# A streaming-encoder block with seven products in its up projection: moves between partition groups issued by GpSimd, turns and taps placed some blocks later

## The reference

```
h = rmsnorm(x, g_ffn_pre[l])
u = causal_dwconv(h @ w_up[l], ffn_conv_w[l])
gate, val = jnp.split(u, 2, axis=-1)
x = x + rmsnorm((jax.nn.silu(gate) * val) @ w_down[l], g_ffn_post[l])
```

## Time and profile before

| | us |
|---|---|
| median of 3 runs | 1702.69 |
| lowest, highest | 1702.57, 1703.47 |
| the profiled execution | 1708.27 |
| its span, first to last instruction | 1706.2 |
| TensorE busy in the span | 1648.2 |
| VectorE busy | 1094.3 |
| ScalarE busy | 834.0 |
| GpSimd busy | 54.2 |

### The profile page before, as it was taken

The page is one execution under the profiler, slowest core; times in us unless marked ns, Lnnn a source line. Parts: engine busy times, 40 slices in busy tenths (PEclk is TensorE's granted clock), DMA queues, the critical chain, the costliest instruction groups (busy, mean ns, idle before and its releaser), DMA issues.

```text
span 1706.2 us, 22099 instructions
## 1 busy us (share of the span) xinstructions
PE 1648.2 (97%) x7219; PEld 1344.5 (79%) x7219; DVE 1094.3 (64%) x1500; ACT 834.0 (49%) x1075; POOL 54.2 (3%) x117
## 2 busy tenths in 40 slices
PE   9999999999999999999999988988889899999998
PEld 7888888888888888888888766766667688888886
DVE  5655566555666676666666777777787777753544
ACT  6644344444444444444456555554545555543432
POOL 2500000000000000000000000000000000000000
PEclk9999999999999999999999999999999999999999
DMA  8877767777666756766664655655556577755653
GB/s 281 274 219 220 195 180 208 213 220 209 189 205 191 260 186 199 235 215 215 227 217 136 192 176 173 206 175 172 176 170 208 163 236 232 246 190 178 210 195 137
DMA packets 207792, 346.81 MB, mean 203 GB/s; under 512 B 28953, under 2 KB 52330, under 8 KB 207210
## 3 DMA queue, kind: packets, MB, share of 16 engines
q1 hardware_dynamic: 201033, 342.48, 64.5%
q0 software_dynamic: 2048, 2.10, 0.4%
q10 hardware_dynamic: 4640, 1.33, 0.3%
HBM read 318.02 MB, written 2.10 MB: 188 GB/s over the span
## 4 chain that ended last, share of the span: by engine, by line
PE 78%; SPq 8%; DVE 4%; DMA 4%; issue 3%; ACT 2%; DVEq 0%; ACTq 0%; POOL 0%; POOLq 0%
PE PS L1679 21%; PE PS L1680 21%; PE PS L1681 21%; SPq L507 7%; DMA raw<-in_w_up_dram 3%; PE PS L1811 3%; PE PS L1813 3%; PE PS L1812 3%; DVE w_lo L1586 2%; ACT w_hi L1005 2%; SPq L522 1%; PE PS L1895 1%; PE PS L1896 1%; PE PS L1897 1%; DVE value_conv L1432 1%
## 5 line engine op out<-in xcount | busy, mean ns | idle before, releaser
L1098 DVE TENSOR_TENSOR w_lo<-raw,w_hi 128x1024 fp32r<-128x1024 f32 x439 | 534.8, 1224 | 451.5 <-ACT w_hi L653 450.3
L653 ACT ACTIVATE w_hi<-raw 128x1024 fp32r<-128x1024 f32 x439 | 462.3, 1059 | 535.4 <-PE PS L1681 453.7
L1679 PE MATMUL PS<-w_hi,hT_hi 128*128 128x512 f32 x1312 | 516.8, 394 | 6.5 <-DVE w_lo L1586 6.4
L1680 PE MATMUL PS<-w_lo,hT_hi 128*128 128x512 f32 x1312 | 511.5, 390 | 0.0
L1681 PE MATMUL PS<-w_hi,hT_lo 128*128 128x512 f32 x1312 | 511.5, 390 | 0.0
L1679 PEld LDWEIGHTS PS<-w_hi,hT_hi 128*128 128x128 f32 x1312 | 246.3, 188 | 72.2 <-DVE w_lo L1586 16.7
L1681 PEld LDWEIGHTS PS<-w_hi,hT_lo 128*128 128x128 f32 x1312 | 246.4, 188 | 52.2
L1680 PEld LDWEIGHTS PS<-w_lo,hT_hi 128*128 128x128 f32 x1312 | 246.5, 188 | 48.6
L1586 DVE TENSOR_TENSOR w_lo<-raw,w_hi 128x1024 fp32r<-128x1024 f32 x136 | 164.9, 1218 | 70.0 <-ACT w_hi L1005 70.0
L1005 ACT ACTIVATE w_hi<-raw 128x1024 fp32r<-128x1024 f32 x136 | 136.7, 1048 | 75.5 <-DMA raw<-in_w_up_dram 50.2
L1679 PE MATMUL PS<-w_hi,act_hi 128*128 128x512 f32 x336 | 131.0, 390 | 0.0
(11 more groups left out here) (251 smaller groups left out, 1807.7 us busy)
## 6 DMA issues: line engine op xcount, KB each, us to landing
raw<-in_w_up_dram SPq DMA_DIRECT2D x176, 512.0 KB, 4.0
raw<-in_w_in_dram SPq DMA_DIRECT2D x112, 512.0 KB, 4.1
raw<-in_w_gate_dram SPq DMA_DIRECT2D x96, 512.0 KB, 4.6
raw<-in_w_down_dram SPq DMA_DIRECT2D x88, 512.0 KB, 4.4
raw<-in_w_mem_kv_dram SPq DMA_DIRECT2D x32, 512.0 KB, 6.3
raw<-in_w_o_dram SPq DMA_DIRECT2D x32, 512.0 KB, 4.5
up_moved<-up_stage SPq DMA_DIRECT2D x352, 32.0 KB, 2.8
raw<-in_w_conv_out_dram SPq DMA_DIRECT2D x16, 512.0 KB, 3.7
```

The lines of the kernel that those rows point to most:

```text
L653: nc.scalar.activation(w_hi[i % RING][:], raw[i % RING][:], ACT.Copy).then_inc(hi_ready, inc)
L1098: nc.vector.tensor_tensor(w_lo[i % RING][:], raw[i % RING][:], w_hi[i % RING][:].bitcast(F32), ALU.subtract).then_inc(lo_ready, inc)
L1679: nc.tensor.matmul(o, a_hi, b_hi, start=first, stop=False, skip_group_check=onto)
L1680: nc.tensor.matmul(o, a_hi, b_lo, start=False, stop=False, skip_group_check=onto)
```

## The change

All moves of the up projection leave SyncE's queue and are issued by GpSimd: chunk 0 written out, chunks 1 to 10 in a hardware loop, each half as one group of 16 DMAs behind its two waits. SyncE's loop has loads alone. In the fast chunks the turns, taps, product and rounding are done behind other units: the product and `act_lo` of chunk `jp` leave the round of `j` and are done at the start of the next one, where they are `value_done(jp - 1, 6)` and `(jp - 1, 7)`. Chunk 9 does those of chunk 7. The silu of the gate, the gate's evacuation and the value's first tap stand behind units 8 and 9.

```diff
@@ fast_step, the loads @@
                 for m, (kb, half) in enumerate(((0, 0), (0, 1), (1, 1), (1, 0))):
                     fast_load(j, m, m - 3 if first else (-4, -3, -2, 0)[m], kb, half)
-                    move_squares(jp, 0, m)
                 for m in range(4, 2 * CB):
                     half, kb = (0, m - 2) if m < CB + 2 else (1, m - CB)
                     fast_load(j, m, (3, 5, 6, 6)[m - 4] if m < 8 else m, kb, half)
-                    if CB <= m < CB + P // SQ:
-                        move_squares(jp, 1, m - CB)
@@ GpSimd @@
+            def move_squares(j, half):
+
+                pool.wait_ge(up_out, 2 * j + half + 1)
+                if not isinstance(j, int):
+                    pool.sem_inc(norm_pace, 1)
+                    pool.wait_ge(up_turned, 2 * j + half - 1)
+                    pool.sem_inc(norm_pace, 1)
+                for a in range(P // SQ):
+                    for m in range(P // SQ):
+                        pool.dma_start(up_moved[half][SQ * m:SQ * (m + 1), a, :, :].rearrange("p q n -> p (q n)"),
+                                       up_stage[half][SQ * a:SQ * (a + 1), m, :, :, :].rearrange("p b t n -> p (b t n)")).then_inc(up_in[half], 16)
+
+            move_squares(0, 0)
+            move_squares(0, 1)
+            with pool.Fori(1, NUP) as j:
+                move_squares(j, 0)
+                move_squares(j, 1)
@@ ScalarE, up_step of chunk 9 @@
                         split(n, i, up_landed(j, i))
+                        if jp == FAST_END - 1 and i == 1:
+                            value_done(jp - 1, 7)
                         gate_done(jp, i)
@@ ScalarE, fast_step @@
-                    if s in (1, 4):
-                        gate_done(jp, {1: 3, 4: 6}[s])
-                    if s in (6, 10):
-                        value_done(jp, {6: 3, 10: 7}[s])
-                    if s == 8:
+                    if s == 1 and not first:
+                        value_done(jp - 1, 7)
+                    if s in (5, 8):
+                        gate_done(jp, {5: 3, 8: 6}[s])
+                    if s == 9:
                         up_evacuate(j, 0)
+                        value_done(jp, 3)
@@ VectorE, up_step of chunk 9 @@
+                        if jp == FAST_END - 1 and i in (1, 2):
+                            value_done(jp - 1, i + 5)
@@ VectorE, fast_step @@
-                    if s in (0, 2, 3):
-                        gate_done(jp, {0: 2, 2: 4, 3: 5}[s])
-                    if s in (5, 7, 8, 9, 11):
-                        value_done(jp, {5: 2, 7: 4, 8: 5, 9: 6, 11: 7}[s])
+                    if s in (0, 2) and not first:
+                        value_done(jp - 1, {0: 6, 2: 7}[s])
+                    if s in (4, 6, 7):
+                        gate_done(jp, {4: 2, 6: 4, 7: 5}[s])
+                    if s in (8, 10, 11):
+                        value_done(jp, {8: 2, 10: 4, 11: 5}[s])
```

21 lines of the change are left out of this document (1 added, 20 removed).

## The result

The changed kernel takes 1679.76 us (median of four executions, 1678.81 to 1681.73) beside 1702.63 us for the kernel before (four, 1701.0 to 1703.47). The ratio is 0.9869, with an interval of 0.9856 to 0.9881: 22.9 us faster. The prediction was 1658.0 with a range of 1651 to 1676. The direction was right and the size was not: half of the gain that was worked out is there, and the time lies above the range.

A forecast was written before the change was run, and what follows sets the result against it. TensorE, 97% busy, was taken to wait 39.0 us before Y, seven times. Savings of 5.4 (head), 36.4 (six rounds) and 2.9 (eighth chunk), 44.7 in all, from the median 1702.69 gave 1658.0 us, range 1651 to 1676.

The forecast's parts named there:

- the clock "kept" behind 2.5 us: TensorE's clock behind the shortened wait before Y: taken to stay up, so Y to u7 takes 9.4 us, not 10.7.
- the last piece of a round: From the end of u16 to Y in the up projection: 12.9 us before, predicted at 9.3.
- "nothing" for chunks 9 to 11: Chunks 9 to 11 and the down projection: no TensorE wait today, so no change in time was predicted.
- Y: First product with a summed left operand in a round; TensorE waits there for w_lo, predicted to fall from 5.6 to 2.5 us.
- the 2.6 us a round: Gain from the queue alone: 2.0 us before Y, half a us at the value turn; as a rival 1684 us, chance 0.13.
- the middle piece: From u7 to the end of u16, ten whole blocks: 28.8 us before, predicted at 27.3 without a wait.
- The rival with GpSimd as the bound: GpSimd's 32 DMAs a round set the pace, making the round longer from 1.64 us a DMA; chance 0.04.
- u16: Tenth of the twelve whole blocks u7 to u18 of a round; its end, predicted 36.7 us behind Y, starts the last piece.
- the 46.3: Predicted us from Y to Y, for 52.37 before: 46.0 by pieces plus 0.3 for load landings.
- the layout: A round planned on paper from Y = 0, engine by engine: pieces of 9.4, 27.3 and 9.3 us, 46.0 in all.
- the row at 963.07: A TensorE wait of 2.07 us in the profile before, with one slow matmul behind it; grounds for taking the clock as kept.
- the rival named: Clock rival: 2.5 us of wait lowers TensorE's clock, 1.3 to 1.7 us more a round, 1667 to 1670 us; chance 0.15.

The follow-up runs named there:

- the filled kernel: The changed kernel with eight more matmuls between X and Y in the seven rounds from the second chunk on, their results unread; 1675.23 us.

## Why the prediction was partly right

The bound, both parts of the change and their direction were right; the size was off by 21.8 us. The steps that failed, in the prediction's own terms: the clock "kept" behind 2.5 us (5.5 us: 4.1 in the six rounds, 1.4 in the last chunk), the end of the program, which was put at nothing without a reason (5.2), the saving taken from the median and not from the execution that it was read from (5.9), the last piece of a round (2.9 with what the middle adds), and "nothing" for chunks 9 to 11 (2.5). The first two are shown by experiments, the last two are read from traces, and the cause of the 5.9 is open.

- **What bounds the kernel.** Right. The wait before Y fell, and the time with it; no other engine took the wait over.
- **The moves on GpSimd.** Right in its prices: 0.50 us an issue (497 ns in the row above), 3.1 to land, and no turn waited for a move. The moves alone were worth more than the 2.6 us a round that the text gave them, 4.2: they also free the middle piece, and they take 2.5 us from the last one and not 2.0. The Trainium skill, DMA: Bandwidth & Descriptors, section Issuing engines are not separate DMA queues, calls what another issuing engine saves usually small beside the DMA itself; here it is 23.7 us of 1709, since four issues stood ahead of a load on the path. The rival with GpSimd as the bound needed 1.64 us a DMA and is out. The 3.1 us for one DMA beside a copy that it drew from the Trainium skill, SBUF — State Buffer, section SBUF: two separate sides, were not seen beside the two-input passes of this kernel.
- **The reordering.** The twelve blocks run without a wait but for 0.2 us ahead of the first; the ten of the middle piece take 27.4 us for 27.3. VectorE waits for ScalarE 45.9 us in the six rounds from 1006 to 1290, 7.7 a round, just under the 8 that the text named as the mark of a wrong layout.
- **The last piece.** 9.7 us for 9.3. On VectorE's timeline of the changed kernel the chain starts late:

```profile
1186.71 1.66 DVE L1429 SCALAR_TENSOR_TENSOR value_conv<-turned_sb,up_taps,value_conv 128x254 f32 x4
1188.29 1.22 DVE L1585 TENSOR_TENSOR w_lo<-raw,w_hi 128x1024 fp32r<-128x1024 f32 x1
...
1195.00 1.22 DVE L1585 TENSOR_TENSOR w_lo<-raw,w_hi 128x1024 fp32r<-128x1024 f32 x1
```

  From the first remainder at 1188.29 to the end of the last at 1196.22 are 7.93 us, and 7.9 were laid out. But it starts 1.68 us behind the end of u16 and not 1.5, because the last tap ends only then. With the clock kept the round is 46.79, which is 0.5 above the 46.3: 2.9 us in six rounds. In the filled kernel the last piece is 9.7 us in the three rounds where raw3 lands in time, 0.4 over the layout, of which the late tap is 0.2 and a slip in the layout 0.1 (its Y stands at 46.1, its pieces add up to 46.0). In the other three it takes 9.8 to 10.5, since ScalarE starts on raw3 5.3 to 5.8 us behind the end of u16. The layout had put the limit at 4.9 and allowed 0.3 a round for such landings; they cost 0.25. The longest of them (u16 ends at 1136.55):

```profile
1142.31 2.01 ACT L1001 ACTIVATE w_hi<-raw 128x1024 fp32r<-128x1024 f32 x2 [4.50 <-DMA raw<-in_w_up_dram]
```

- **The clock.** Here the step failed as a judgement. "At 2.5 us I take the clock as kept, by the row at 963.07" rested on one wait in one profile. That wait of 2.07 us stands in all twenty profiles of this study at the same place, since the change doesn't touch it, and in nine of them the clock fell behind it. So the row had only shown one of its two outcomes. The window behind it, and two around the 2.32 us before Y of chunk 2, in the changed kernel beside the experiments:

```profile
963.00:967.00 4.00, 4.00 (x11) 0.57 0.77 199
1005.00:1009.00 4.00, 1.68 (x7) 1.00 0.00 0
1009.00:1013.00 4.00, 3.50 (x15) 1.00 0.58 164
```

  There the shorter wait lowered the clock and the longer one did not; in the profile from the comparison it was the other way round, 0.80 us for the first matmul at 1006.74. Behind the waits of 2.7 us and more in the later rounds it fell each time, in all three profiles of the changed kernel; behind the 2.77 us before Y of chunk 2 in the kernel with the moves alone, shown above, it did not (Y to u7 in 9.44 us). It costs 0.7 us a round: 4.1 in six rounds and 5.05 in all seven, against 1.3 to 1.7 a round that the rival named. A chance of 0.15 for it was too low by far.
- **The last chunks.** From Y of chunk 8 to the first block of chunk 9 are 43.6 us for 42.2, 1.4 more, again behind a slow clock. "Chunks 9 to 11 run without a wait of TensorE today ... nothing" failed too. In chunk 9 of the changed kernel TensorE waits twice, 1.7 us in all, for remainders. The product, act_hi and act_lo of chunk 7 stand at the start of this chunk, and the timelines of TensorE, ScalarE and VectorE show how they hold it up:

```profile
1341.96 0.51 PE L1680 MATMUL PS<-w_hi,hT_hi 128*128 128x512 f32 x1 [1.14 <-DVE w_lo L1095]
1345.53 0.50 PE L1680 MATMUL PS<-w_hi,hT_hi 128*128 128x512 f32 x1 [0.52 <-DVE w_lo L1095]
```

```profile
1338.64 1.06 ACT L973 ACTIVATE act_hi<-value_conv 128x1024 fp32r<-128x1024 f32 x1 [3.46 <-DVE value_conv L1458]
```

```profile
1340.68 1.23 DVE L1095 TENSOR_TENSOR w_lo<-raw,w_hi 128x1024 fp32r<-128x1024 f32 x1 [2.07 <-ACT w_hi L647]
1341.82 1.22 DVE L1461 TENSOR_TENSOR act_lo<-value_conv,act_hi 128x1024 fp32r<-128x1024 f32 x1
```

  ScalarE stands 3.46 us for VectorE's product, because act_hi comes ahead of the next w_hi in its queue; VectorE then stands 2.07 us for that w_hi, and its remainder is late for TensorE. Behind the second wait are act_lo and the gate's turn. The "some 10 us of room" were VectorE's over the whole chunk; at its start a pass of one engine stands ahead of what the other needs, and there is none. From the first block of chunk 9 to the last matmul the changed kernel loses some 2.5 us.
- **The end of the program.** It was missing from the sum: 5.2 us, the wait of 5.7 us for 0.5. The list of what a moved step costs had its issues and its landings, not what the engine's closing drain costs.
- **The baseline.** "The loss per round is in both, so I subtract from the median" failed. The saving was read from an execution that took 1708.27, and it was taken from 1702.69. The experiments show the kernel before at 1706 to 1711 on three chips and, on the one where both kernels ran, a gain of 28 to 29 us; in the comparison the changed kernel took the same 1680 and the gain was 22.9. Taken from 1708.27, the prediction would have been 1663.6. Why the kernel before has two times is open, as told above.

The sum of the misses inside the trace: rounds 4.1 by the clock and 2.9 by the last piece and what the middle adds, last chunk 1.4, chunk 9 and later 2.5, the end 5.2, less 0.3 at the head (Y of chunk 2 at 1006.74 for 1007.0): 15.8 of the 16 us.

## What to carry to other kernels

When a program moves DMA issues to an engine that had few, read its last records and what the other engines wait for at the very end, and let that engine's program end early if they wait for it. When a wait of the matrix engine is shortened, don't credit the clock behind it before several waits of about the new length, in several executions, are seen to leave it up; a few matmuls for nothing ahead of the wait are a cheap test, and they must stand ahead of every semaphore on which that wait hangs. And take a saving that is read from one profiled execution from that execution's own time, since other executions of the same kernel can lie 6 us away for a reason that its profile doesn't show.

## What the hardware showed that was not expected

- GpSimd's drain at the end took 5.29 us with 64 DMAs issued, 3.98 with 240, and 10.52 with 416 to 448, the same to 0.01 us in every profile that has GpSimd at work to the end. In the changed kernel it starts 230 us after the last DMA and still takes its 10.52; straight behind the last move it took 11.72 in two kernels and 12.88 in the filled one.
- Whether TensorE's granted clock falls behind a short wait differs from one execution to the next. Behind the same wait of 2.07 us it fell in nine of twenty profiles; behind 2.32 us it fell in one of three of the changed kernel; behind 2.77 us it stayed up once, in the kernel with the moves alone.
- Matmuls whose results nobody reads made the changed kernel faster by 5.05 us and the kernel before by 6.6. The same matmuls 4.5 us later in the same wait made the latter slower by 29.
- The kernel before took 1701 to 1703.5 us in the comparison and 1706.3 to 1710.8 in 54 executions on three chips. The changed one took 1679 to 1682 in the comparison and in both later groups of runs. The cause is not known.
